# Starting the output projection inside the attention by scaling the convolution half instead of the attention half

## The reference

```python
def rms_norm(x, g):
    xf = x.astype(jnp.float32)
    y = xf * lax.rsqrt(jnp.mean(xf * xf, axis=-1, keepdims=True) + EPS)
    return (y * g.astype(jnp.float32)).astype(x.dtype)
...
    mix = jnp.concatenate([rms_norm(attn, p["g_out_attn"]), rms_norm(c, p["g_out_conv"])], axis=-1)
    x = x + rms_norm(mix @ p["w_out"], p["g_post_mix"])
```

## Time and profile before

| | |
|---|---|
| median of 3 runs | 1808.64 us (1808.14 to 1814.15) |
| profiled execution | 1805.88 us, span 1804.1 us |
| TensorE busy | 1725.5 us, 96% |
| VectorE busy | 1139.0 us, 63% |
| ScalarE busy | 881.5 us, 49% |
| mean granted TensorE clock | 0.991 |

### The profile page before, as it was taken

The page is one execution under the profiler, slowest core; times in us unless marked ns, Lnnn a source line. Parts: engine busy times, 40 slices in busy tenths (PEclk is TensorE's granted clock), DMA queues, the critical chain, the costliest instruction groups (busy, mean ns, idle before and its releaser), DMA issues.

```text
span 1804.1 us, 30507 instructions
## 1 busy us (share of the span) xinstructions
PE 1725.5 (96%) x12168; PEld 1602.9 (89%) x12168; DVE 1139.0 (63%) x2095; ACT 881.5 (49%) x1656; POOL 2.2 (0%) x12
## 2 busy tenths in 40 slices
PE   7999999889997999999999889999999999999998
PEld 6999999756665899988878889999999999999998
DVE  5499997686674677633556677654576633676533
ACT  6322222655664666554456555543545433555533
POOL 0000000000000000000000000000000000000000
PEclk9999999999998999999999999999999999999999
DMA  7233222345223444444443344444444544444443
GB/s 239 64 117 111 82 84 97 117 164 206 83 83 103 137 148 142 152 130 129 135 147 105 95 117 137 135 139 132 137 140 148 154 132 139 138 138 146 143 135 105
DMA packets 349219, 233.74 MB, mean 130 GB/s; under 512 B 7979, under 2 KB 322465, under 8 KB 349071
## 3 DMA queue, kind: packets, MB, share of 16 engines
q1 hardware_dynamic: 342907, 220.24, 40.3%
q10 hardware_dynamic: 6172, 11.55, 1.8%
HBM read 220.68 MB, written 11.50 MB: 129 GB/s over the span
## 4 chain that ended last, share of the span: by engine, by line
PE 82%; DVE 8%; ACT 6%; issue 3%; ACTq 1%; DMA 0%; DVEq 0%
PE bank L1184 76%; PE bank L1181 7%; ACT whi L594 1%; DVE wlo L1747 1%; DVE op_lo L1734 1%; DVE Y L1734 1%; ACT wide L608 1%; DVE Sx L2085 1%; DVE XT L2097 1%; DVE op_x L2100 1%; DVE cv L1734 1%; DVE Pp L2025 0%; ACT Pp L811 0%; DVE Pp L1738 0%; DVE Sy L2078 0%
## 5 line engine op out<-in xcount | busy, mean ns | idle before, releaser
L1184 PE MATMUL bank<-op_hi,whi 128*128 128x352 f32 x1632 | 540.4, 331 | 13.9 <-DVE op_lo L1734 9.0
L1747 DVE TENSOR_TENSOR wlo<-raw,whi 128x1024 fp32r<-128x1024 f32 (+1 forms) x312 | 373.6, 1199 | 243.9 <-ACT whi L594 243.6
L1184 PE MATMUL bank<-op_hi,wlo 128*128 128x352 f32 x1632 | 526.3, 322 | 0.0
L1184 PE MATMUL bank<-op_lo,whi 128*128 128x352 f32 x1632 | 525.7, 322 | 0.0
L594 ACT ACTIVATE whi<-raw 128x1024 fp32r<-128x1024 f32 (+1 forms) x312 | 325.2, 1043 | 288.4 <-DMA raw<-in_w_up_dram 78.5
L1184 PEld LDWEIGHTS bank<-op_hi,whi 128*128 128x128 f32 x1632 | 308.4, 189 | 23.6 <-issue 19.2
L1184 PEld LDWEIGHTS bank<-op_lo,whi 128*128 128x128 f32 x1632 | 309.3, 190 | 0.5
L1184 PEld LDWEIGHTS bank<-op_hi,wlo 128*128 128x128 f32 x1632 | 308.1, 189 | 0.0
L1184 PE MATMUL bank<-fhi,whi 128*128 128x352 f32 x528 | 171.2, 324 | 0.0
L1184 PE MATMUL bank<-fhi,wlo 128*128 128x352 f32 x528 | 170.7, 323 | 0.0
L1184 PE MATMUL bank<-h1hi,whi 128*128 128x352 f32 x480 | 159.7, 333 | 3.0 <-DVE h1lo L1734 3.0
(11 more groups left out here) (276 smaller groups left out, 2326.6 us busy)
## 6 DMA issues: line engine op xcount, KB each, us to landing
raw<-in_w_up_dram SPq DMA_DIRECT2D x132, 512.0 KB, 3.8
raw<-in_w_down_dram SPq DMA_DIRECT2D x48, 512.0 KB, 3.8
raw<-in_w_out_dram SPq DMA_DIRECT2D x24, 512.0 KB, 3.9
raw<-in_w_xq_dram SPq DMA_DIRECT2D x24, 512.0 KB, 3.8
raw<-in_w_xo_dram SPq DMA_DIRECT2D x24, 512.0 KB, 3.8
raw<-in_w_in_dram SPq DMA_DIRECT2D x20, 512.0 KB, 3.7
raw<-in_w_down_dram SPq DMA_DIRECT2D x24, 384.0 KB, 3.4
cached<-in_cache_win_k_dram SPq DMA_DIRECT2D x8, 1024.0 KB, 6.3
```

The costliest lines, as they stand in the source:

```text
L1184: return pe.matmul(out, lhsT, rhs, start=first, stop=last, skip_group_check=shared)
L1747: dve.tensor_tensor(wlo[v % SLOTS][:, 0:nk, :], raw[v % SLOTS][:, 0:nk, :], whi[v % SLOTS][:, 0:nk, :].bitcast(F32), ALU.subtract).then_in ...
```

## The change

The common factor is moved. With r the root of the attention half's mean square (plus epsilon), the old operand is [attn / r, c]; the new one is [attn, c * r], which is r times the old one. The post-norm divides by the root of the mean square, so r cancels, except for its epsilon, which becomes epsilon * r * r. `add_root` adds 8 * epsilon * r * r to `Sy` once per chunk, and the post-norm's root then has a zero bias. `att_scale` with its reciprocal is gone; `mix_scale` multiplies the four tiles of C by r. There is one root buffer per chunk.

The attention half of the operand needs no root now. So its high and low parts are made inside the last attention steps, k-tile by k-tile, and the first three units' matmuls on it (`mix_tile`) are put between the last attention steps' own matmuls; the fourth unit's are put between unit 0's matmuls on the convolution half. Four units are then open at once, in banks 0, 1, 7 and 6. The Sqrt table is loaded ahead by a small root (`warm`). The samples' slots end one step earlier.

```diff
-    STDA = mn("STDA", 37376, [P, CW])
-    RSCA = [mn(f"RSCA{i}", 61440 + 1408 * i, [P, CW]) for i in range(CH)]
+    STDA = [place(f"STDA{i}", TAB + 1408 * i, [P, CW]) for i in range(CH)]
...
+    EARLY_OUT = 4
...
-        return 3 * s if s < EARLY else min(3 * EARLY - (-(2 * SAMPLE - 3 * EARLY) * (s - EARLY) // (NP - EARLY)), 2 * SAMPLE)
+        return 3 * s if s < EARLY else min(3 * EARLY - (-(2 * SAMPLE - 3 * EARLY) * (s - EARLY) // (NP - 1 - EARLY)), 2 * SAMPLE)
...
+    def out_bank(t):
+        return (0, 1, 7, 6)[t] if t < EARLY_OUT else t % 2
...
+        def mix_attended(c, m):
+            act.activation(op_hi[SLOT["mix", c]][:, m, :], ATT[:, m, c * CW:(c + 1) * CW], ACT.Copy, scale=g_of("g_out_attn", m)).then_inc(*mark("op_hi", ("mix", c, m)))
+
+        def att_square(j, k):
+            c, n = CONV_ORDER[j], j * AT + k
+            if n >= 4:
+                act.wait_ge(*at("asq_used", n - 4))
+            act.activation(SQA[n % 4][:, :], ATT[:, k, c * CW:(c + 1) * CW], ACT.Square).then_inc(*mark("asq", n))
...
+            if s == NP - 1:
+                act.wait_ge(*at("score", (s, parts_of(STEPS[s][0]) - 1, 1)))
+                act.wait_ge(*at("satt", (1, 3, 1)))
+                for k in range(2):
+                    act.wait_ge(*at("att", NP - AT + k))
+                    mix_attended(2, k)
             if s < NP:
                 probabilities(s)
+            if s == NP:
+                act.activation(sd[:, 3:4], eps[:, :], ACT.Sqrt).then_inc(*mark("warm", 1))
+                for k in range(2):
+                    att_square(0, k)
+                act.wait_ge(*at("att", NP - 2))
+                mix_attended(2, 2)
+                att_square(0, 2)
...
         def att_root(j):
...
-        att_squares(0)
...
+        def mix_convolved(c, m):
+            act.wait_ge(*at("cg", (c, m)))
+            act.activation(op_hi[SLOT["mix", c]][:, AT + m, :], C[:, m, c * CW:(c + 1) * CW], ACT.Copy, scale=g_of("g_out_conv", m)).then_inc(*mark("op_hi", ("mix", c, AT + m)))
+
+        act.wait_ge(*at("att", NP - 1))
+        att_square(0, 3)
+        mix_attended(2, 3)
         att_root(0)
...
-            act.activation(sd[:, 0:3], bank[6][:, CW:CW + 3], ACT.Sqrt, bias=eps_d[:, :], scale=1.0 / (D * D)).then_inc(*mark("root", key))
+            act.activation(sd[:, 0:3], bank[6][:, CW:CW + 3], ACT.Sqrt, bias=0.0 if key[0] == "out" and key[2] == "y" else eps_d[:, :],
+                           scale=1.0 / (D * D)).then_inc(*mark("root", key))
...
+        def mix_tile(t, k):
+            u, b = XFIRST + t, out_bank(t)
+            if k == 0:
+                take(b, "y", XU[t])
+                pe.wait_ge(*at("w_lo", u))
+            pe.wait_ge(*at("op_lo", ("mix", 2, k)))
+            w, s = u % SLOTS, SLOT["mix", 2]
+            hi, lo = op_hi[s][:, k, :], op_lo[s][:, k, :]
+            mm(bank[b][:, 0:CW], whi[w][:, k, :], hi, k == 0, False)
+            mm(bank[b][:, 0:CW], whi[w][:, k, :], lo, False, False)
+            ins = mm(bank[b][:, 0:CW], wlo[w][:, k, :], hi, False, k == NT - 1)
+            if k == NT - 1:
+                ins.then_inc(*mark("unit", u))
+
         for s in range(LAST_STEP + 1):
+            if s == NP + 1:
+                for t in range(EARLY_OUT - 1):
+                    mix_tile(t, 2)
...
             if 0 <= s - 2 < NP:
                 product(s - 2)
+            if s == NP:
+                for t in range(EARLY_OUT - 1):
+                    mix_tile(t, 0)
             sample(*sample_slot(s, 0))
             if 0 <= s - 1 < NP:
                 turn_p(s - 1, 0)
+            if s == NP:
+                for t in range(EARLY_OUT - 1):
+                    mix_tile(t, 1)
...
         att_mean(0)
+        for t in range(EARLY_OUT - 1):
+            mix_tile(t, 3)
+        for k in range(AT):
+            mix_tile(EARLY_OUT - 1, k)
+            mix_tile(0, AT + k)
...
+            if 0 < t < EARLY_OUT:
+                for k in range(AT, NT):
+                    mix_tile(t, k)
             w = u % SLOTS
-            for k in range(NT):
+            for k in range(NT if t >= EARLY_OUT else 0):
...
+            if s == NP + 1:
+                mix_low(2, 2)
...
+            if s == NP - 1:
+                for k in range(2):
+                    mix_low(2, k)
...
-        def att_scale(j):
+        def mix_scale(j, k):
             c = CONV_ORDER[j]
             dve.wait_ge(*at("asd", j))
-            dve.reciprocal(RSCA[j][:, :], STDA[:, :]).then_inc(*mark("ars", j))
-            dve.wait_ge(*at("ars", j))
-            for k in range(AT):
-                cols = ATT[:, k, c * CW:(c + 1) * CW]
-                dve.tensor_tensor(cols, cols, RSCA[j][:, :], ALU.mult).then_inc(*mark("an", (c, k)))
-
-        att_scale(0)
-
-        def mix_low(c, m):
+            cols = C[:, k, c * CW:(c + 1) * CW]
+            dve.tensor_tensor(cols, cols, STDA[j][:, :], ALU.mult).then_inc(*mark("cg", (c, k)))
+
+        def mix_conv_low(c, m):
...
+        mix_low(2, 3)
+        mix_scale(0, 0)
+        for k in range(1, AT):
+            mix_scale(0, k)
+            mix_conv_low(2, k - 1)
+        mix_conv_low(2, AT - 1)
...
+        def add_root(c):
+
+            j = CONV_ORDER.index(c)
+            r = STDA[j][:, :]
+            dve.wait_ge(*at("cg", (c, AT - 1)))
+            stt(r, r, 8.0 * EPS, r, ALU.mult, ALU.mult).then_inc(*mark("ars", c))
+            dve.wait_ge(*at("ars", c))
+            dve.wait_ge(*at("ysum", ("out", c, 1)))
+            dve.tensor_tensor(Sy[:, :], Sy[:, :], r, ALU.add).then_inc(*mark("ysum", ("out", c, "e")))
...
+            if name == "out" and m == 1:
+                add_root(c)
```

More of the change, by code:

```diff
@@ L837, in _ @@
         act.wait_ge(*at("v_out", TT))
[L838 to L841, removed]
-            for k in range(AT):
[L843 to L846, removed]
         def att_root(j):
             act.wait_ge(*at("asq_used", j * AT + AT - 1))
-            if j:
-                act.wait_ge(*at("ars", j - 1))
-            act.activation(STDA[:, :], bank[5 - j % 2][:, 0:CW], ACT.Sqrt, bias=eps[:, :]).then_inc(*mark("asd", j))
-        att_squares(0)
-        att_root(0)
-        def mix_low(c, m):
[L859 to L863, removed]
+            act.activation(STDA[j][:, :], bank[5 - j % 2][:, 0:CW], ACT.Sqrt, bias=eps[:, :]).then_inc(*mark("asd", j))
+        def mix_convolved(c, m):
[4 more added lines that the diff above has]
+        mix_attended(2, 3)
+        att_root(0)
         def square_y(name, c, m, src):
@@ L995, in _ @@
         for m in range(AT):
-            mix_low(2, m)
+            mix_convolved(2, m)
         for t in range(NX):
@@ L1001, in _ @@
             if t in (2, 3):
-                att_squares(t - 1)
+                for k in range(AT):
+                    att_square(t - 1, k)
                 att_root(t - 1)
@@ L1029, in _ @@
             chains_middle(t)
-            evac_y(name, c, m, u, t % 2, name != "xq")
+            evac_y(name, c, m, u, out_bank(t), name != "xq")
             split_to(u + 3)
@@ L1033, in _ @@
                 for k in (0, 1):
-                    mix_low(0, 2 * (t - 3) + k)
+                    mix_attended(0, 2 * (t - 3) + k)
+                    mix_convolved(0, 2 * (t - 3) + k)
             if t - 24 in range(2 * MT):
@@ L1039, in _ @@
                     act.wait_ge(*at("unit", unit_of[FREE["mix", 1]]))
-                mix_low(1, t - 8)
+                mix_attended(1, t - 8)
+                mix_convolved(1, t - 8)
             if 0 <= t - MEMK0 < 2 * BD:
@@ L1631, in _ @@
         att_mean(0)
+        for t in range(EARLY_OUT - 1):
+            mix_tile(t, 3)
+        for k in range(AT):
+            mix_tile(EARLY_OUT - 1, k)
+            mix_tile(0, AT + k)
         for t in range(NX):
             name, c, m = XU[t]
-            u, b = XFIRST + t, t % 2
+            u, b = XFIRST + t, out_bank(t)
             src = "mix" if name == "out" else name
             s = SLOT[src, c]
-            take(b, "y", (name, c, m))
-            pe.wait_ge(*at("w_lo", u))
-            if m == 0:
+            if t >= EARLY_OUT:
+                take(b, "y", (name, c, m))
+                pe.wait_ge(*at("w_lo", u))
+            if m == 0 and t:
                 pe.wait_ge(*at("op_lo", (src, c, NT - 1)))
@@ L1651, in _ @@
                     between(t, 0)
-            ins.then_inc(*mark("unit", u))
+            if t >= EARLY_OUT:
+                ins.then_inc(*mark("unit", u))
             if t in (2, 3):
@@ L2030, in attended, with mix_low @@
             dve.tensor_copy(ATT[:, hp, i * P:(i + 1) * P], bank[product_bank(s)][:, 0:P]).then_inc(*mark("att", s))
+        def mix_low(c, m):
+            s = SLOT["mix", c]
+            dve.wait_ge(*at("op_hi", ("mix", c, m)))
+            stt(op_lo[s][:, m, :], ATT[:, m, c * CW:(c + 1) * CW], g_of("g_out_attn", m), op_hi[s][:, m, :].bitcast(F32), ALU.mult, ALU.subtract).then_inc(*mark("op_lo", ("mix", c, m)))
         for s in range(LAST_STEP + 1):
+            if s == NP + 1:
```

(12 more changed lines are left out.)

4 lines of the change are left out of this document (removed).

## The result

The change makes the kernel slightly slower: 1814.39 us (20 runs, 1811.72 to 1819.18) against 1808.86 us (20 runs), a ratio of 1.0027 with a 95% interval of 1.0018 to 1.0036. That is 5.5 us by the medians. It lies inside the 0.5% that I had called no change, but 0.9 us above my range. The profiled execution took 1813.42 us. Beside the first four experiments one of the 35 runs of the kernel before took 2422.9 us at a granted clock of 0.654; it is left out of the ratios.

The account below looks back on a forecast made before the run. TensorE bounds the kernel, its largest hole being 9.02 us idle before the first projection matmul. 1.6 - 4.8 + 2.7 + 0.25 = -0.25 us, so no change: 1808 us, range 1800.5 to 1813.5.

Parts of the forecast that it names:

- A: Start of the last score matmuls, 548.1 us before; forecast 1.6 us later, ends 0 and 2.6.
- B: End of the fifth projection unit, 598.67 us before; A to B forecast near 48 us, before 50.6.
- Step 7: Sample windows tightened ahead of the last scores: last pair step about 9.0 us, A 1.6 us later.
- Step 6: Half clock on TensorE behind the two new gaps: 2.7 us given back, ends nothing or 6.8 us.
- Steps 1 and 2: Last two head pairs and last transposes: last probabilities start at A+3.75, ScalarE's last copy ends at A+11.6.
- Step 3: Third k-tile ahead of the last attention product: TensorE idle 4.1 us, the product queued behind this wait.
- Step 5: Second chunk's squares behind unit 4's weight split: TensorE idle 3.2 us, load 5.6; unit 4 done 4.8 us less than before.
- Step 8: Epsilon operations on VectorE, paid for the third chunk, just ahead of the split at 664.30: 0.25 us.
- The slower one: Last product behind early tiles, clock low after both gaps: loses 6.8 us, 1812 us; slower by 3 to 9 us, 0.11.
- The attention pays more: Tighter windows meet a late cache load or samples' softmax: A 4 us or more later; 0.04 together with the clock.
- The hand-over works: Hole before the first projection closes: 4 to 9 us less, 0.20; over 9, 0.10; all 10.8 us gone gives 1798.

Follow-up runs that it names:

- the first four experiments: As listed: slots only; the change with the old slots; squares first; product first. Measured 1815.26, 1809.85, 1807.92 and 1807.43 us.
- squares first: The change with ScalarE's squares of the second and third chunk put ahead of the weights' high parts: 1807.92 us, ratio to before 0.9990.
- product first: The change with the third k-tile's matmuls behind the last attention product and its high part ahead of the table load: 1807.43 us, ratio to before 0.9986.
- slots only: The kernel before with one edit, the samples' slots ending one step earlier: 1815.26 us, ratio 1.0029.
- its repaired form: The change with old slots, product first and squares first together, 1797.52 us; also the new order, 1796.13 us in its second run.
- the new order: The change's arithmetic with old slots, early matmuls put into existing gaps, squares ahead of weight splits: 1797.20 us, again 1796.13 us.

## Why the prediction was wrong, point by point

I forecast -0.25 us as 1.6 - 4.8 + 2.7 + 0.25. The trace has 4.5 + 2.0 + 0.3 = 6.8, and 0.7 us more that lies ahead of 362 us and so ahead of everything changed. Term by term, against my own: 4.5 for 1.6 (A), 5.9 for 2.7 (the clock), 3.9 less for 4.8 less (the rest between A and B, of it 1.0 the longer second gap), 0.3 for 0.25. The medians differ by 5.5 us.

- **Step 7 failed, the start A.** I priced the tighter slots at 1.6 us, ends 0 and 2.6. They cost 4.5 us in each of the three traces with new slots and no low stretch near 400 us, and 4.5 to 6.0 by the medians. I had looked at the last head pairs alone. There the estimate was nearly exact: 8.93 us between the last two pairs' second scores, forecast 9.0. What I left out was the pairs before: at the second scores of the last pair but one the change is already 4.3 us late, for which I had only the 2.2 us of the moved product. (By the step's own terms, these 2.2 and the 0.25 by which the last pair grows, A comes 2.5 us later and not 1.6.) I argued that moving work to where TensorE is full gains nothing and costs only its own length. But the moved piece brings VectorE work with it, and TensorE then waits 2.6 us more for VectorE in earlier pairs (the waits' 4.2 less the 1.65 ahead of A, 2.02 for 0.37).
- **Step 6, the clock, was mis-sized.** I took 2.7 us. Measured: 1.7 us lost at A (the scores 2.05 for 1.13, the second transposes 1.80 for 1.04), behind a 2.02 us gap that the slots made, for which step 7 had the wait and step 6 no clock; 1.7 behind the 4.1 us gap (the low stretch of 3.4 us); and 2.5 on the second mean. That is 5.9 us, near the end of 6.8 that I had kept. The first 1.7 are partly chance, since they did not come in the trace of squares first.
- **Steps 1 and 2 held but for that.** The last probabilities started at A + 5.3 instead of A + 3.75. The 1.5 us between them are the half clock at A.
- **Step 3 held.** The gap ahead of the third k-tile was forecast as 4.1 us and is 4.12, with the last product queued behind. The table load with what follows took 1.30 us from start to start here too, not the 2.66 of the Trainium skill's page "ScalarE: Activation LUTs", section "What ACT_TABLE_LOAD costs".

```profile
566.40 1.28 ACT L850 ACT_TABLE_LOAD   x1
567.70 0.20 ACT L850 ACTIVATE sd<-eps 128x1 f32<-128x1 f32 x1
```

- **Step 5 held in kind.** The second gap is where it was forecast, behind the weight split: 4.23 us instead of 3.2, the load 6.4 instead of 5.6. The chip showed something more: each of these two gaps was worth 6.5 to 7.0 us when it was mended, more than its 4.2 us, because the half clock behind it went with it (and with the product first the second gap shrank too).

```profile
590.09 1.06 ACT L597 ACTIVATE whi<-raw 128x1024 fp32r<-128x1024 f32 x1 [3.70 <-DMA raw<-in_w_out_dram]
591.05 1.64 ACT L816 ACTIVATE SQA<-ATT 128x352 f32<-128x352 f32 x4
```

- **Step 8 is not tested.** From B to the end the change takes 0.3 us longer, forecast 0.25. But slots only, with the old arithmetic, takes 0.2 us longer there, and squares first, with the new, takes none. Traces differ by more than this term.
- **The rivals.** The slower one (6.8 us lost to half clock, 1812 us) had the right mechanism, and its condition, a loss of over 3 us, was met. It lacked the slots. "The attention pays more", A 4 us or later, came true: 4.5 us by the trace from 362 us on. I had called it small because no wait for a cache load showed. The cause I named first was the wrong one. The second, the samples' softmax, is 1.4 us of the waits by name; the copies of the sample output ahead of A, in my step 7 but not in this rival, are behind the longest. I had given this rival, together with the clock, 0.04. "The hand-over works" is not what the change does, but it is what its repaired form does: forecast 1798 us if all 10.8 us of hole went, measured 1797.5 and 1796.1.

## What to carry to other kernels

Starting the next stage inside the last one paid here only where its instructions went into gaps that were already there, behind whatever the critical chain needs next on each queue: nine matmuls ahead of the last product and four squares behind a weight split each cost 6.5 to 7 us. A schedule that is tightened by one step has to be priced over all the steps it tightens, and by the engines that share its work, not by its last step alone. When a large hole is closed and the time does not fall, look for the half clock behind each of the smaller gaps that took its place.

## What the runs showed of the hardware that I had not expected

A gap of about 2 us can be followed by a low stretch of clock or not, with the same instructions. Six kernels have the same gap of 2.02 or 2.03 us just ahead of A. In five the granted clock fell behind it (the last scores took 1.57 to 2.08 us), and in one, squares first, it did not, so they took 1.13 us in full, though the five kernels made from the change are the same up to there:

```profile
553.15 1.32 PE L1197 MATMUL bank<-ident,Pp 128*128 128x128 f32 x8 [2.02 <-DVE Pp L2074]
...
554.40 1.13 PE L1200 MATMUL bank<-KT,QT 64*128 64x512 f32 x4
```

One kernel, the new order, did both. Its two executions have a gap of 1.79 and 1.78 us near 720 us. Behind the first the granted clock was 0.50 and the same six matmuls took 1.25 us, behind the second 0.80 us:

```profile
720.04 1.25 PE L1198 MATMUL bank<-ones_d,Sx 128*128 128x1 f32 x6 [1.79 <-DVE Sx L2151]
```

```profile
719.95 0.80 PE L1198 MATMUL bank<-ones_d,Sx 128*128 128x1 f32 x6 [1.78 <-DVE Sx L2151]
```

All twelve traces have a gap of 2.06 us near 400 us and one of 2.1 us in the post-norm chain. Each of the two was followed by a low stretch in four.

The low stretches read 0.50, and one of 3.4 us over busy matmuls costs 1.7 us. Whether one comes behind a given gap is partly chance, which gives one profiled execution an error of some microseconds against the median. Between A and B the gap of 9.0 us was followed by one in both traces that have it, every gap above 2 us was too, and those of up to 1.75 us by none. The rule of the Trainium skill's page "TensorE: Matmul & The Clock Gate", section "Why this matters for your kernels", that gaps between bursts are to be avoided, agrees with these traces. The Trainium skill's page states it for longer gaps than these; here gaps of 1.8 and 2.0 us were already followed by half clock.
